# Split-fp32 products with features on the output partitions: three 256-column matmuls into one PSUM sum, in place of a 512-column and a 256-column matmul

## The reference, cut to what matters

```python
y = h @ w                        # h: 256 tokens x 2048, w: 2048 x width, in many places
# the experts, as the kernel computes them: all 16384, with a gate that is zero where one was not picked
hidden = gelu(h @ u.T)           # 256 x 16384
out = (hidden * gate) @ v        # 256 x 2048
```

## Time and profile before

| | |
|---|---|
| median of three runs | 5155.08 us (5152.84 to 5158.27) |
| the profiled execution's own time | 5148.11 us |
| its span, first to last instruction | 5146.5 us |
| TensorE matmuls busy | 4087.7 us, 79% |
| weight loads busy | 3428.4 us, 67% |
| DVE busy | 2836.7 us, 55% |
| ACT busy | 1634.7 us, 32% |
| mean granted TensorE clock | 0.883 of full speed |

### The profile page before, as it was taken

One profiled execution on the slowest core, in us unless ns is written; L12 is line 12 of the kernel. 1 busy time (PEld: TensorE's weight loads), 2 busy tenths in 40 slices (PEclk: granted clock), 3 DMA queues, 4 the chain that ended last, 5 costly groups with the idle time before them and its releaser, 6 DMA issues. The chain is left out here.

```text
span 5146.5 us, 60867 instructions
## 1 busy us (share of the span) xinstructions
PE 4087.7 (79%) x21154; PEld 3428.4 (67%) x21154; DVE 2836.7 (55%) x3932; ACT 1634.7 (32%) x2007; POOL 133.2 (3%) x133
## 2 busy tenths in 40 slices
PE   7876778860589999999999679748847888985668
PEld 6663367750478888888888568536747777873557
DVE  4578755457855555555555455345555555535344
ACT  3210043320244444444444233223221133322133
POOL 0000000000510000000000000000000000000000
PEclk9988889985799999999999889758969999987689
DMA  5432244330256666665665335203400044541024
GB/s 175 128 100 88 77 138 142 118 98 0 98 179 203 211 198 193 208 203 186 209 204 185 113 124 185 83 0 111 150 0 0 0 144 146 181 137 34 5 78 164
DMA packets 190460, 642.91 MB, mean 125 GB/s; under 512 B 24632, under 2 KB 37176, under 8 KB 188992
## 3 DMA queue, kind: packets, MB, share of 16 engines
q1 hardware_dynamic: 175440, 611.12, 36.4%
q0 software_dynamic: 2304, 20.97, 1.1%
q10 hardware_dynamic: 12528, 8.13, 0.6%
HBM read 621.26 MB, written 18.89 MB: 124 GB/s over the span
## 5 line engine op out<-in xcount | busy, mean ns | idle before, releaser
L1507 DVE TENSOR_TENSOR weights_trailing<-weight_ring,weights_leading 128x1024 fp32r<-128x1024 f32 x512 | 624.4, 1225 | 594.9 <-ACT weights_leading L1471 594.0
L368 DVE TENSOR_TENSOR weights_trailing<-weight_ring,weights_leading 128x1024 fp32r<-128x1024 f32 x536 | 647.4, 1223 | 428.7 <-ACT weights_leading L363 428.7
L363 ACT ACTIVATE weights_leading<-weight_ring 128x1024 fp32r<-128x1024 f32 x536 | 567.5, 1060 | 786.4 <-PE lin_in_acc L430 351.2
L1471 ACT ACTIVATE weights_leading<-weight_ring 128x1024 fp32r<-128x1024 f32 x512 | 539.3, 1060 | 681.2 <-PE dense_down L1461 348.5
L1439 PE MATMUL dense_up<-pe_parts,weights_leading 128*128 128x512 f32 x2048 | 722.8, 400 | 22.1 <-DVE weights_trailing L1507 15.9
L430 PE MATMUL lin_in_acc<-lin_in_parts,weights_leading 128*128 128x512 f32 x1728 | 607.7, 401 | 37.8 <-DVE weights_trailing L368 37.8
L1461 PE MATMUL dense_down<-weights_leading,dense_act_parts 128*128 128x512 f32 x2048 | 630.5, 389 | 0.0
L1439 PE MATMUL dense_up<-pe_parts,weights_trailing 128*128 128x256 f32 x2048 | 554.4, 281 | 0.0
L430 PE MATMUL lin_in_acc<-lin_in_parts,weights_trailing 128*128 128x256 f32 x1728 | 469.7, 282 | 0.0
L1439 PEld LDWEIGHTS dense_up<-pe_parts,weights_leading 128*128 128x128 f32 x2048 | 379.3, 189 | 115.5 <-issue 19.5
L1461 PEld LDWEIGHTS dense_down<-weights_leading,dense_act_parts 128*128 128x128 f32 x2048 | 384.5, 188 | 79.6
(11 more groups left out here) (521 smaller groups left out, 5792.9 us busy)
## 6 DMA issues: line engine op xcount, KB each, us to landing
weight_ring<-in_w_experts SPq DMA_DIRECT2D x512, 512.0 KB, 4.2
weight_ring<-in_w_in SPq DMA_DIRECT2D x216, 512.0 KB, 4.3
weight_ring<-in_w_out SPq DMA_DIRECT2D x112, 512.0 KB, 4.3
weight_ring<-in_w_att SPq DMA_DIRECT2D x64, 512.0 KB, 4.3
weight_ring<-in_w_key SPq DMA_DIRECT2D x32, 512.0 KB, 3.6
weight_ring<-in_w_value SPq DMA_DIRECT2D x32, 512.0 KB, 3.6
weight_ring<-in_w_query SPq DMA_DIRECT2D x32, 512.0 KB, 4.2
weight_ring<-in_w_o SPq DMA_DIRECT2D x32, 512.0 KB, 4.4
```

The source lines that it names most:

```text
L363: self.nc.scalar.activation(leading, x, ACT.Copy).then_inc(self.led, 1)
L368: return self.nc.vector.tensor_tensor(trailing, x, leading.bitcast(F32), ALU.subtract)
L1471: nc.scalar.activation(ring.leading[:, b], ring.ring[:, b], ACT.Copy).then_inc(split_led, 1)
L1507: v.tensor_tensor(ring.trailing[:, b], ring.ring[:, b], ring.leading[:, b].bitcast(F32), ALU.subtract).then_inc(ring.split, 1)
```

## The change

In `linear`, for feature-major products, the pair becomes three matmuls of 256 columns, all into the same 256 columns of PSUM. Two sub-blocks now share a bank, so a tile takes 2 banks in place of 4, and only the first matmul of an even sub-block carries `start`. DVE takes a tile with one operation. Token-major products keep their three matmuls; the reversal of their order in the last block goes.

In `dense_experts` the first product gets the same form and its accumulator two alternating sets of 2 banks (`up[:, n % 2]`), so its wait is now for the tile before the last. `lower` and `add` go, with their buffer and semaphores; the gelu reads PSUM directly and stands behind piece 1 of the next tile; the gate's multiplication and the split stand behind piece 3.

```diff
@@ linear @@
-        acc = s.ps("acc", [P, 2, 4 if not tokens else TILES, WIDE])
+        acc = s.ps("acc", [P, 2, TILES, WIDE] if tokens else [P, 2, 4, SEQ])
...
-        taken, added = s.sem("taken"), s.sem("added")
+        taken = s.sem("taken")
...
-                                    pairs = [(high[:, here], feat.rearrange("p a t -> p (a t)"), acc[:, half, sub]),
-                                             (low[:, here], feat[:, 0], acc[:, half, sub, 0:SEQ])]
-                                if end:
-
-                                    pairs.reverse()
-                                for m, (still, moving, out) in enumerate(pairs):
-                                    mm = nc.tensor.matmul(out, still, moving,
-                                                          start=begin and m == 0, stop=end and m == len(pairs) - 1)
+                                    pairs = ((high[:, here], feat[:, 0]), (high[:, here], feat[:, 1]), (low[:, here], feat[:, 0]))
+
+                                    begin = begin and sub % 2 == 0
+                                for m, (still, moving) in enumerate(pairs):
+                                    mm = nc.tensor.matmul(acc[:, half, sub], still, moving, start=begin and m == 0,
+                                                          stop=end and m == 2, skip_group_check=not tokens)
...
                     if residual:
-                        v.tensor_tensor(out, out, acc[:, half, :, 0:SEQ], ALU.add).then_inc(added, 1)
+                        v.tensor_tensor(out, out, acc[:, half], ALU.add).then_inc(taken, 1)
                     else:
-                        v.tensor_copy(out, acc[:, half, :, 0:SEQ]).then_inc(added, 1)
-
-                    dve.wait_ge(added, n + 1)
-                    v.tensor_tensor(out, out, acc[:, half, :, SEQ:], ALU.add).then_inc(taken, 1)
+                        v.tensor_copy(out, acc[:, half]).then_inc(taken, 1)
@@ dense_experts @@
-        up, down = s.ps("up", [P, 4, WIDE]), s.ps("down", [P, 2, TILES, WIDE])
+        up, down = s.ps("up", [P, 2, 4, SEQ]), s.ps("down", [P, 2, TILES, WIDE])
...
-                                    pe.wait_ge(summed, g * 8 + (2 * n + sub // 2 + 1))
+                                    pe.wait_ge(curved, g * 8 + (2 * n + sub // 2 + 1))
...
-                                    high = (ring.leading[:, b, j, cols], feat.rearrange("p a t -> p (a t)"), up[:, sub])
-                                    rest = (ring.trailing[:, b, j, cols], feat[:, 0], up[:, sub, 0:SEQ])
-                                    pairs = (rest, high) if end else (high, rest)
-                                    for m, (still, moving, to) in enumerate(pairs):
-                                        mm = nc.tensor.matmul(to, still, moving, start=begin and m == 0, stop=end and m == 1)
+                                    pairs = ((ring.leading[:, b, j, cols], feat[:, 0]), (ring.leading[:, b, j, cols], feat[:, 1]),
+                                             (ring.trailing[:, b, j, cols], feat[:, 0]))
+                                    for m, (still, moving) in enumerate(pairs):
+
+                                        mm = nc.tensor.matmul(up[:, n % 2, sub], still, moving,
+                                                              start=begin and m == 0 and sub % 2 == 0,
+                                                              stop=end and m == 2, skip_group_check=True)
...
-                def lower(g, n):
+                def curve(g, n):
                     for q in range(2):
                         if q == 0:
                             act.wait_ge(upped, g * 4 + (n + 1))
                         else:
                             act.wait_ge(ring.freed, piece(g, n * 8 + 7)[0] + 1)
-                        nc.scalar.activation(low[:, q], up[:, 2 * q:2 * q + 2, SEQ:], ACT.Copy).then_inc(lowed, 1)
-
-                def curve(g, n):
+
+                        act.wait_ge(gated, g * 8 + (2 * n + q + 1))
+                        nc.scalar.activation(act_in[:, q], up[:, n % 2, 2 * q:2 * q + 2], ACT.Gelu_apprx_tanh).then_inc(curved, 1)
+
+                def lead_activations(g, n):
                     for q in range(2):
-                        act.wait_ge(summed, g * 8 + (2 * n + q + 3))
-                        nc.scalar.activation(act_in[:, q], act_in[:, q], ACT.Gelu_apprx_tanh).then_inc(curved, 1)
-                    for q in range(2):
-                        act.wait_ge(gated, g * 8 + (2 * n + q + 1))
+                        act.wait_ge(gated, g * 8 + (2 * n + q + 3))
...
-                            if c == 2:
-                                lower(g, n - 1)
-                            if c == 4:
+                            if c == 1:
                                 curve(g, n - 1)
+                            if c == 3:
+                                lead_activations(g, n - 1)
...
-                def add(g, n):
-                    for q in range(2):
-                        dve.wait_ge(lowed, g * 8 + (2 * n + q + 1))
-                        v.tensor_tensor(act_in[:, q], low[:, q], up[:, 2 * q:2 * q + 2, 0:SEQ], ALU.add).then_inc(summed, 1)
-
...
-                            if c == 2:
-                                add(g, n - 1)
-                            if c == 4:
+                            if c == 3:
                                 weigh(g, n - 1)
```

More of the change, by code:

```diff
@@ L419, in _ @@
                                 if tokens:
-                                    pairs = [(feat[:, 0, here], high, acc[:, half, sub]),
-                                             (feat[:, 1, here], high, acc[:, half, sub]),
-                                             (feat[:, 0, here], low, acc[:, half, sub])]
-                                else:
-                                    pairs = [(high[:, here], feat.rearrange("p a t -> p (a t)"), acc[:, half, sub]),
-                                             (low[:, here], feat[:, 0], acc[:, half, sub, 0:SEQ])]
-                                if end:
-                                    pairs.reverse()
-                                for m, (still, moving, out) in enumerate(pairs):
-                                    mm = nc.tensor.matmul(out, still, moving,
-                                                          start=begin and m == 0, stop=end and m == len(pairs) - 1)
+                                    pairs = ((feat[:, 0, here], high), (feat[:, 1, here], high), (feat[:, 0, here], low))
+                                else:
+                                    pairs = ((high[:, here], feat[:, 0]), (high[:, here], feat[:, 1]), (low[:, here], feat[:, 0]))
[3 more added lines that the diff above has]
+                                                          stop=end and m == 2, skip_group_check=not tokens)
                         mm.then_inc(ring.freed, 1)
@@ L1393, in dense_experts @@
     with Stage(nc, "dense") as s:
-        up, down = s.ps("up", [P, 4, WIDE]), s.ps("down", [P, 2, TILES, WIDE])
+        up, down = s.ps("up", [P, 2, 4, SEQ]), s.ps("down", [P, 2, TILES, WIDE])
         gate = s.sb("gate", [P, SEQ, TOPK])
-        low, act_in, act_out = (s.sb(x, [P, 2, 2, SEQ]) for x in ("low", "act_in", "act_out"))
+        act_in, act_out = (s.sb(x, [P, 2, 2, SEQ]) for x in ("act_in", "act_out"))
         act_parts = s.sb("act_parts", [P, TOPK, 2, SEQ], F32R)
-        gate_used, upped, lowed, summed, curved, gated, led, ready, emptied, taken, cleared = (
-            s.sem(x) for x in ("gate_used", "upped", "lowed", "summed", "curved", "gated", "led", "ready", "emptied",
-                               "taken", "cleared"))
+        gate_used, upped, curved, gated, led, ready, emptied, taken, cleared = (
+            s.sem(x) for x in ("gate_used", "upped", "curved", "gated", "led", "ready", "emptied", "taken", "cleared"))
         gate_here, split_led = s.sem("gate_here"), s.sem("split_led")
@@ L1519, in weigh @@
                         at = 4 * n + 2 * q
-                        dve.wait_ge(curved, g * 8 + (2 * n + q + 1))
+                        dve.wait_ge(curved, g * 8 + (2 * n + q + 5))
                         v.tensor_tensor(act_out[:, q], act_in[:, q], gate[:, :, at:at + 2].rearrange("p t n -> p n t"),
@@ L1538, in _ @@
                 dve.wait_ge(emptied, 1)
-                dve.sem_inc(summed, 2)
+                dve.sem_inc(curved, 4)
+                dve.sem_inc(gated, 2)
                 dve.sem_inc(taken, 1)
```

## The result

The changed kernel took 5181.3 us (median of five runs, 5172.7 to 5184.8) against 5155.1: 1.0047 times the time before, 95% interval 1.0032 to 1.0061. It is 26 us slower; forecast were 39 us less, and the range ended at 5181. The profiled execution took 5176.1 us by its own time, 28 us more than the profiled one of before.

A forecast was written before the change was run, and what follows sets the result against it. The prediction took TensorE's own matmul rate to bound the changed stages. Savings of 12, 17.6 and 9.1 us summed to 39 us less, from the median of 5155.1 to 5116 us, with a range of 5052 to 5181.

The forecast's parts named there:

- Part 1: Feature-major linears and experts' first product: three narrow matmuls cost 350 ns against a pair's 352, 12 us less over 6048.
- rival with the fixed price: Same products: each matmul pays 13.3 ns over its columns, a triple costs 360 ns, 5177 us in all; chance 0.2.
- column case: Same products: the excess goes with the columns, a triple costs 340 ns, 5055 us in all; chance 0.14.
- Part 2: Ends of the fourteen linears: one DVE operation for a tile saves 1.26 us each, 17.6 us less.
- Part 3: Experts' first product: the alternating accumulator removes a 0.38 us wait at 24 tile borders, 9.1 us less.
- Part 4: Experts: the copies and additions removed from ACT and DVE and the moved gelu cost no time.
- rule on the busy share of loads: Changed products: loads busy 87% cannot grow by half, so a triple takes 459 ns, 650 us more; the prediction rejected it.

The follow-up runs named there:

- e6: Kernel before, with the 256-column matmul of the experts' first product as two of 128 columns with the same stationary: 5361.5 us, ratio 1.0404.
- e3: Kernel before, with the matmuls of a sub-block ordered wide, wide, narrow, narrow in linear and the experts' first product: 5136.9 us against 5154.7, ratio 0.9968.
- e5: Kernel before, with linear's matmuls ordered 8 wide then 8 narrow for a piece, experts unchanged: 5140.6 us against 5156.9, ratio 0.9965.
- e1: Kernel before, with only linear in the new form and the old dense_experts: 5173.2 us against 5154.7, ratio 1.0035.
- e2: Kernel before, with only dense_experts in the new form and the old linear: 5162.3 us, ratio 1.0016.
- e4: Kernel before, with each 512-column matmul of the experts' second product as two of 256 columns: 5223.0 us against 5156.9, ratio 1.0126.
- e7: Kernel before, with three narrow matmuls and one DVE operation only in the last tile of thirteen of fourteen linears: 5171.2 us against 5156.9, ratio 1.0025.
- e8: Kernel before, with order wide, wide, narrow, narrow in linear and experts' first product, plus the narrow last tile in thirteen linears: 5158.1 us, ratio 0.9998.

## Why the prediction was wrong

**Part 1 failed: the cost of a narrow matmul.** "The cost of a narrow matmul in a stream is the distance from its start to the next. ... Three steps add to 0.35 us, so the new triple costs 350 ns against 352". The rows were read rightly and are not the cost. In the mixed stream a part of the narrow matmul's time stood in the distance behind the wide one; e6 shows this at its plainest (59 and 286 ns recorded), and e3 and e5 show that a pair comes near 346.7 ns once the order changes, so the wide ones carry hardly a price of their own. The rows held a warning: a pair of 352 less the 226.7 ns of an even wide step leaves 125 ns for the narrow one, not 117. In an even stream the step is 120.0 ns, in the changed kernel, in e1, e2, e4 and e7. The term was 12 us less and is 48 us more (6048 x 8 ns): 60 of the 65 us between forecast and result, and the sign. The argument that was held to matter most, two narrow ones in succession in 0.23 us, has the same flaw: both their neighbours were wide.

**The rival with the fixed price had the cost of a triple right**, 360 ns, and its 5177 us stand against a median of 5181. That they are so near is in part luck, since the sum below leaves 8 us open; and e6 shows that a fixed price of 13.3 ns does not hold at 128 columns. It was given 0.2. What spoke for it were the even steps of the second product, the only stream of one width in the trace; they were named as a bound and passed over for rows that looked nearer. They were nearer in shape and taken in a stream of another kind.

**The column case is refuted**: a step of 113 ns at 256 columns was reached in no even stream, and e4 shows 120 with columns unchanged.

**Part 2 held.** 1.26 us at each end, 17.6 us in all, as the rows of the last end show. From the last matmul of a linear to the first of the next stage it is 1.4 us in most of them, a little more.

**Part 3 held and was a little short**: 12 us for 9.1, since the slow step behind the wait went as well, which was left at nothing with 2.6 us as its bound.

**Part 4 held.** No wait of TensorE on ACT, DVE or weights came up in the experts, beside the one for the stage's first piece.

**The sum by the measured terms** is 48 - 17.6 - 12 = 18 us more, of 26. The rest of some 8 us was also in e1 and e2 and is not in the changed products. The short stages between them (norms, attention) moved by 1 to 5 us each in both directions from one trace to the other, and the kernel before ranged from 5144.5 to 5167.9 us in these comparisons. What of the 8 us is the change's stays open.

**The rule on the busy share of loads** (the Trainium skill, Perfetto Trace Analysis, "Identifying the Most-Contended Engine") pointed the right way, but what the prediction made of it had the wrong size: the share went from 87% to 240.00 of 240.00 us, and the triple costs 360 ns and not 459. The loads overlap one another in the record (0.19 us each, 0.12 us apart), so the busy share of 87% left room for almost half as many again.

## What to carry to other kernels

Take the price of a matmul from a stream of one width, or as the sum over a whole period; never from the distance of two starts where wide and narrow alternate. An fp32r matmul of 256 or 512 columns cost its columns at 2.4 GHz and 13.3 ns here, and one of 128 columns about 114 ns. So 512 columns in one go save 13.3 ns over two halves, and a form that gives this up must earn it back: at a stage's end it did (1.26 us against 64 x 8 ns), in the middle it did not. When a change moves code ahead of a loop, look at the loop's first microseconds after its jump back, and at the number of instruction packets, before the time is put down to the change itself.

## What was not expected of the hardware

- **The order of like matmuls matters.** The same matmuls cost 352 ns a pair in alternation and 348 as two wide and two narrow (e3) or eight and eight (e5), 18 and 16 us for the kernel. The gain is the same with half of the changes and with an eighth. Why alternation costs this is open.
- **A floor of about 114 ns for a matmul with its load** (e6; 112 ns for single columns in the kernel before), while the record gives each load 0.19 us and shows loads of 120 ns distance without a gap. That it is the load that sets the floor is the likely reading; no matmul without a load was there to compare.
- **A loop's place among the instructions.** The experts' loop lost 4 to 5 us in each of its seven returns with 704 instructions more ahead of it, by a stall of 2 to 4 us behind its fifth matmul and, at most of them, the lower clock; 512 more cost nothing. The stalls end 1.2 to 1.6 us after a 16 KB packet of instructions, so they are waits for the fetch. The likely reading of the place is that in e7 and e8 a packet ends just behind the loop's first instructions, so that the next one is wanted at once: 512 is two packets of 256 instructions, 704 is not a whole number of them. In e4 the stall stood right at the jump, though the loop starts at the same place: the fetch of its first packet began about 2.4 us later against the array than before. That TensorE works through its instructions faster there, 120 ns a matmul in place of 227, and leaves the fetch less of a lead, is a reading that no run tests.
